# Delta-rule mixer of a three-block network on one core: chunks of 128 tokens in natural order instead of 64 folded ones

## The chip, the cores and the metric

The kernel runs on one core of one Trainium2 chip. The metric is the time of one execution of the whole program on the device, in microseconds (us); smaller is better. The program is written for the engines directly: every engine (TensorE = PE, VectorE = DVE, ScalarE = ACT, GpSimd = POOL, SyncE = SP) has its own list of instructions, carried out in that order, and semaphores join the lists. A wait in a list holds back all that stands behind it.

## The reference

The reference is a network of width 1024 on 256 tokens in float32: a block with a gated-delta-rule mixer and a mixture of 32 experts, then an "even" and an "odd" layer. The change touches only the first mixer. Its recurrence, run forward and, on reversed inputs, backward over the tokens, with 16 value heads of width 128 that share 8 query/key heads in pairs:

```python
def _gated_delta_rule(q, k, v, beta, g):
    """S_t = exp(g_t)(I - b_t k_t k_t^T) S_{t-1} + b_t k_t v_t^T ; o_t = S_t^T q_t.  Chunked WY form."""
    gc = jnp.cumsum(g, axis=-1)                       # within a chunk
    decay = jnp.exp(jnp.where(incl, gc[..., :, None] - gc[..., None, :], -jnp.inf))
    kb = k * beta[..., None]
    lhs = eye + jnp.einsum("nbhik,nbhjk->nbhij", kb, k) * decay * (1.0 - eye)
    u = solve(lhs, v * beta[..., None])               # unit lower triangular
    w = solve(lhs, kb * jnp.exp(gc)[..., None])
    attn = jnp.einsum("nbhik,nbhjk->nbhij", q, k) * decay
    def step(state, inp):                             # one chunk after the other
        v_new = u_c - w_c @ state
        o = q_c @ state + attn_c @ v_new
        state = state * gl[..., None, None] + k_c^T @ v_new
    ...
o = _gated_delta_rule(q, k, v, beta_f, g_f) + _rev(_gated_delta_rule(_rev(q), ..., _rev(g_b)))
```

q, k and v come from a projection of x, a convolution over 5 tokens and a silu; q and k are made unit vectors. The sum of both directions is normed, gated by silu(z) and projected by `w_out`. The reference cuts the sequence into chunks of 64; the result doesn't depend on the length of a chunk beyond rounding.

## The kernel before

The four stages `gdn`, `moe`, `even`, `odd` follow one another; the change is in `gdn`, the mixer. A head here is one of the 8 query/key heads with its two value heads. Every product is float32, and the profile counts each matmul as two instructions (a transpose as one).

**Tokens.** 256 tokens make 4 chunks of 64. Forward the order is 0, 1, 2, 3, backward 3, 2, 1, 0. Tokens are folded as 0, 3, 1, 2 (in the host's layout of xT and by `chunks` on ScalarE), so that a tile of 128 partitions holds two chunks, and one step of the recurrence takes the forward direction on one half of the partitions and the backward one on the other. A head has 4 such steps (`g.step`), the first with an empty state and the last without a new one.

**What one head costs on TensorE** (`gdn_tensor`, line 441): the projections, `project_half` (449), 12 parts of 4 matmuls, each 128x128 weights and 256 columns; the inverse of the unit triangular matrices by doubling: levels 1 to 4 join blocks of 1, 2, 4, 8 to 16 and 32 with products of 32x32 tiles, `level_y` (477) and `level_z` (500), 32 matmuls each; level 5 joins blocks of 32 to 64 with 16 each. Then the steps: `solve` (530) U = W^T R and `attend` (548), each 4 matmuls of 64x64 weights and 128 columns, 4 times; `add_state` (557), 4 of 64x128 weights and 128 columns, 3 times; `read_state` (520), 4 of 128x64 weights and 256 columns, 3 times. Also `keys` (591: k^T k, k^T q and the transposed keys), `unit_sums` (571), `turn_v` (583), and `turn_out` (605), which transposes the finished output of head h-2.

**Who serves it.** ScalarE (815): `keep_y` copies a level's y out of PSUM, `keep_u` U, `cross` writes level 5's block into W, `silu_v`, `keep_out`, `compact` (copies the diagonal 32x32 blocks of A = `g.at` next to each other), `decay` (the exponentials of the mask), `decay_state`. VectorE (1090): `update` X after each level (after level 4 it also turns X into W by 4 transposes, line 1178), `conv`, `bars` (log-decays less a mask), `triangles` (A = k^T k times decays), `attention`, `inverse_begin`, and in the steps `left`, `state`, `out`, `out_scale` (norm times gate, which `turn_out` waits for). GpSimd (1333) masks A for each level (line 1344).

**Order.** Written out by hand in each engine's loop over h. Iteration h carries the inverse of head h with the steps of head h-1 and `turn_out` of head h-2; the next head's q and k parts are projected two heads ahead. Between two products that depend on each other there stands mostly one projection part. At h = 6 there is no head h+2 left, so its last stretch has no projection. A ninth pass (h = 8) has the steps of head 7, with the first half of the output projection between them (`out_part`, line 787, 16 parts of 4 matmuls); `out_rest` follows (line 802). On VectorE `out_scale(h-2)` stands before `update(h, 4)` (lines 1311 to 1315).

**Queues.** All loads of weights are in SP's queue (`gdn_sync`, 373): units of 1 MB into a ring of 24 slots, each when its slot was used up (`fill`, 240); also the rows of cumulated log-decays, through DRAM (`rows_in`, 398). The experts' weights follow when a list of signals of the inverse is there (line 421).

Of the kernel before, what the change touches and what calls it, by code (L numbers as in the profile page):

```python
# [10 lines left out]
P = 128  # L11
# [94 lines left out]
def constants():  # L106
# [5 lines left out]
    half = P // 2  # L112
    same = i // half == j // half
    ci, cj = (r % half)[:, None], np.arange(half)[None, :]
    side = (r // half)[:, None]
    ordered = lambda before, w: np.where((side + w) % 2 == 0, before(ci, cj), before(cj, ci))

    def level(b):
        def before(u, v):
            return (u // (2 * b) == v // (2 * b)) & ((u // b) % 2 == 0) & ((v // b) % 2 == 1)  # L120
        return np.stack([ordered(before, w) for w in (0, 0, 1, 1)], 1)
# [4 lines left out]
    for w in POOL_WINDOWS:  # L126
# [18 lines left out]
        "eye2": ci == cj, "together": same,  # L145
        "upto": np.stack([ci <= cj, ci >= cj], 1), "behind": np.stack([ci > cj, ci < cj], 1),
        "bars": np.stack([~ordered(lambda u, v: u <= v, w) for w in (0, 0, 1, 1)], 1) * BIG,
        "eye32": (r % 32)[:, None] == np.arange(32)[None, :],
        "levels": np.stack([level(b) for b in LEVELS], 1).reshape(P, len(LEVELS), 4, 2, 32)[r, :, :, r // 32 % 2],
# [15 lines left out]
class Build:  # L165
    def __init__(self, nc, ins, out):
# [10 lines left out]
        self.delta_rows = nc.dram_tensor("delta_rows", (2, 4, QKH, P), F32, kind="Internal").ap()  # L177
# [115 lines left out]
    def gdn(self):  # L293
        al, g, new = self.alloc, Place(), self.signals.of
        H2, M8 = P // 2, [P, 2, 4, P // 2]
# [3 lines left out]
        g.eg, g.epsq = al("eg", [P, 2, 2, 2, VH]), al("epsq", [P, QKH, 2])  # L299
        late = QKH - 1  # L300
        g.cv, g.W, g.att, g.kk, g.vtm = [None] * 3, [None] * 3, [None] * 2, [None] * 2, [None] * 2
        shapes = (("cv", g.cv, [P, 2, T]), ("W", g.W, M8), ("att", g.att, M8), ("kk", g.kk, [P, 3, REP, P]),
# [5 lines left out]
        g.S, g.Sd = al("S", [P, 2, REP, P]), al("Sd", [P, 2, REP, P])  # L308
        g.R, g.U = al("R", [P, REP, P]), al("U", [P, REP, P])
        g.ost, g.junk = al("ost", [P, 4]), al("junk", [P, P])  # L310
        assert self.top <= ARENA - 9 * KT * UC
        for name, of, shape in shapes:
            for n in range(len(of)):
                if n != late % len(of):
                    of[n] = al(f"{name}{n}", shape)
# [9 lines left out]
        g.rowsb = pair("rows", [P, 512])  # L325
# [3 lines left out]
        g.dm, g.at = (al(n, M8) for n in ("dm", "at"))  # L329
        g.ac, g.mt, g.X, g.Y, g.Wc = (al(n, [P, 2, 4, 32]) for n in ("ac", "mt", "X", "Y", "Wc"))  # L330
        g.ktm = al("ktm", [P, 2, P])
# [4 lines left out]
        g.step = ((0, 0), (1, 0), (1, 1), (0, 1))  # L336
# [7 lines left out]
         g.ys, g.zx, g.zw, g.reads, g.us, g.avs, g.adds) = (  # L344
            new("PE", n) for n in ("gates", "gate_sums", "decays_turned", "q_projected", "v0_projected", "z0_projected",
                                   "unit_sums", "v_turned", "keys", "out_turned", "y_product",
                                   "zx_product", "zw_product", "state_read", "u_product", "attn_product",
                                   "state_added"))
        (g.gate_exps, g.gate_ln, g.gate_kept, g.cum_kept, g.qk_kept, g.vr_kept, g.qk_silu, g.v_silu, g.z_silu, g.squared, g.norm_ln, g.norms, g.rates_made, g.z_kept,
         g.v_kept, g.k_kept, g.decays, g.w_crossed, g.y_kept, g.u_kept, g.kk_made, g.s_decayed, g.out_squares, g.out_ln,  # L350
         g.out_norms, self.y_made) = (
            new("ACT", n) for n in ("gate_exps", "gate_ln", "gate_kept", "decays_kept", "qk_kept", "v_raw_kept", "qk_silu", "v_silu", "z_silu",
                                    "squared", "norm_ln", "norms", "rates_made", "z_kept", "v_kept", "k_kept", "decays", "w_crossed", "y_kept",
                                    "u_kept", "keys_scaled", "state_decayed", "out_squares", "out_ln", "out_norms", "y_made"))
# [10 lines left out]
        g.cleared2, g.masked, g.blank = (new("POOL", n) for n in ("w_cleared", "level_masked", "blank_made"))  # L365
# [7 lines left out]
    def gdn_sync(self, g):  # L373
# [19 lines left out]
        for x in range(2):  # L393
            SP.dma_start(self.delta_rows[x].rearrange("c h (v i) -> (c h v) i", v=REP),
                         g.crow[0:64, x * 64:(x + 1) * 64]).then_inc(*g.rows_out.up())
        SP.wait_ge(*g.rows_out(2))

        def rows_in(h):
            for x in range(2):
                SP.dma_start(g.rowsb[h % 2][g.halves[x]].rearrange("p (c n) -> p c n", c=4),  # L400
                             self.delta_rows[x:x + 1, :, h, :].to_broadcast([P // 2, 4, P])).then_inc(
                    *g.rows_in[h % 2].up())
# [18 lines left out]
        for done in (g.zw(QKH), g.w_crossed(QKH), g.v_turned(QKH), g.v_kept(QKH), g.kk_made(3 * QKH), g.x_made(9 * QKH),  # L421
                     g.masked(4 * QKH), g.attn_made(QKH)):
            SP.wait_ge(*done)
# [13 lines left out]
    def chunks(self, a, cc):  # L437

        return a.rearrange("p z (q i) -> p z q i", q=4)[:, :, cc:4 - cc:3 - 2 * cc, :]

    def gdn_tensor(self, g):
# [3 lines left out]
        chunk = lambda x, cc: slice(cc * P + x * 64, cc * P + x * 64 + 64)  # L445
# [31 lines left out]
        def level_y(h, l):  # L477


            if l == 1:  # L480
                M.wait_ge(*g.x_made(9 * h + 1))
                M.wait_ge(*g.k_kept(h + 1))
            else:
                M.wait_ge(*g.x_made(9 * h + 2 * l - 2))
            if l < 5:
                M.wait_ge(*g.masked(4 * h + l))
            for m in range(8):
                cc, w, n = m // 4, m % 4 // 2, slice(m * 32, m * 32 + 32)
# [4 lines left out]
                else:  # L493
                    for x in range(2):
                        a, b = w ^ x, 1 - (w ^ x)
                        q = M.matmul(ps[hq[2 * x + b], 3, n], g.at[hq[2 * x + a], cc, m % 4, 32 * b:32 * b + 32],
                                     g.X[hq[2 * x + a], cc, m % 4], start=True, stop=True, skip_group_check=True)
            q.then_inc(*g.ys.up())

        def level_z(h, l):  # L500
            M.wait_ge(*g.y_kept(5 * h + l))
            if l > 1:
                M.wait_ge(*g.x_made(9 * h + 2 * l - 1))
            elif h > 0:
                M.wait_ge(*g.w_crossed(h))
            for m in range(8):
                cc, w, n = m // 4, m % 4 // 2, slice(m * 32, m * 32 + 32)
# [4 lines left out]
                else:  # L512
                    for x in range(2):
                        a, b = w ^ x, 1 - (w ^ x)
                        q = M.matmul(ps[hq[2 * x + a], 4, n], g.Y[hq[2 * x + b], cc, m % 4],
                                     g.W[h % 3][hq[2 * x + b], cc, m % 4, 32 * b:32 * b + 32], start=True, stop=True,
                                     skip_group_check=True)
            q.then_inc(*(g.zx if l < 5 else g.zw).up())

        def read_state(h, n):  # L520
            cc, w = g.step[n]
            M.wait_ge(*g.s_kept(3 * h + n))
            for z in (1, 0):
                for x in range(2):
                    q = M.matmul(ps[hx[x], 6, (1 - z) * 256:(2 - z) * 256], g.cv[h % 3][:, z, chunk(x, cc)],  # L525
                                 g.S[:, w ^ x, :, :].rearrange("p v e -> p (v e)"), start=True, stop=True,
                                 skip_group_check=True)
            q.then_inc(*g.reads.up())

        def solve(h, n):  # L530
            cc, w = g.step[n]
            if n == 0:
                M.wait_ge(*g.x_made(9 * h + 9))
                M.wait_ge(*g.w_crossed(h + 1))
                M.wait_ge(*g.v_kept(h + 1))
                if h > 0:
                    M.wait_ge(*g.o_made(4 * h))
            else:
                M.wait_ge(*g.r_made(3 * h + n))
                M.wait_ge(*g.o_made(4 * h + n))  # L540
            for v in range(REP):
                for x in range(2):
                    rhs = g.vtm[h % 2][hx[x], cc, v, :] if n == 0 else g.R[hx[x], v, :]
                    q = M.matmul(ps[hx[x], 7, v * P:(v + 1) * P], g.W[h % 3][hx[x], cc, 2 * w + v], rhs, start=True,
                                 stop=True, skip_group_check=True)
            q.then_inc(*g.us.up())

        def attend(h, n):
            cc, w = g.step[n]
            M.wait_ge(*g.u_kept(4 * h + n + 1))  # L550
            for v in range(REP):
                for x in range(2):
                    q = M.matmul(ps[hx[x], 7, 256 + v * P:256 + (v + 1) * P], g.att[h % 2][hx[x], cc, 2 * w + v],
                                 g.U[hx[x], v, :], start=True, stop=True, skip_group_check=True)
            q.then_inc(*g.avs.up())

        def add_state(h, n):
            cc, w = g.step[n]
            if n > 0:
                M.wait_ge(*g.oq_made(3 * h + n))  # L560
            elif h > 0:
                M.wait_ge(*g.oq_made(3 * h))
            M.wait_ge(*g.kk_made(3 * h + n + 1))
            M.wait_ge(*g.u_kept(4 * h + n + 1))
            for v in range(REP):
                for x in range(2):
                    q = M.matmul(bank(5 + (w ^ x), P, v * P), g.kk[h % 2][hx[x], n, v, :], g.U[hx[x], v, :], start=True,
# [23 lines left out]
        def keys(h):  # L591
            cv = g.cv[h % 3]
            M.wait_ge(*g.qk_silu(h + 1))
            if h > 0:
                M.wait_ge(*g.y_kept(5 * h))
            for cc in range(2):
                M.transpose(bank(3, P, cc * P), cv[:, 1, tile(cc)], ident)
            for cc in range(2):
                for x in range(2):
# [2715 lines left out]
```

## Time and profile before

| | |
|---|---|
| median of 3 runs | 1098.59 us (1098.55 to 1101.07) |
| the profiled execution, its own time | 1099.91 us |
| its span, first to last instruction | 1098.6 us |
| TensorE busy | 1040.1 us, 95% of the span, 10605 matmul instructions |
| VectorE, ScalarE, GpSimd busy | 380.0, 353.3, 45.4 us |
| chain that ended last | PE 79%, SP's queue 12%, DVE 3%, ACT 3%, issue 2%, DMA 2% |
| mean granted clock of TensorE | 0.983 of full |

The chain is followed back from the last instruction. Busy time of matmuls is modelled at the ends, since they overlap; where a price is needed, the distance between the starts of two groups is the better measure. All rows below are of this one execution. The gdn stage is the first 403 us or so, the experts reach to about 670 us.

### The profile page before, as it was taken

How to read it: one execution, taken by the hardware profiler on the slowest of the kernel's cores; microseconds unless marked ns; L12 is line 12 of the kernel's file. 1: busy time of each engine (PE TensorE's matmuls, PEld its weight loads, DVE VectorE, ACT ScalarE, POOL GpSimd, SP SyncE). 2: the span in 40 equal slices, each digit the busy share in tenths (PEclk: the TensorE clock that was granted, in tenths of full speed). 3: DMA queues.
4: the chain of work that ended last, by engine and by line, in shares of the span. 5: the costliest groups of instructions: out<-in, count | busy, mean ns of one | idle time of the engine just before them, and what ended most of it. 6: DMA issues, size and time to landing. Idle time of an engine off the chain costs nothing.

```text
span 1098.6 us, 24280 instructions
## 1 busy us (share of the span) xinstructions
PE 1040.1 (95%) x10605; PEld 789.5 (72%) x10605; DVE 380.0 (35%) x942; ACT 353.3 (32%) x1006; POOL 45.4 (4%) x48
## 2 busy tenths in 40 slices
PE   9999999999989999889667899999999999999998
PEld 6777777777767787434333388888888888877787
DVE  2555556655644225101000234532000120065551
ACT  3555456555555232110000113022111331133550
POOL 0110010010000000000000000000000000024000
PEclk9999999999989999989888999999999999999999
DMA  7242232331323777999999953443444334472221
GB/s 282 57 162 83 92 131 80 120 131 75 118 81 121 299 306 281 398 421 420 423 422 423 406 230 137 155 154 115 153 153 153 135 121 149 136 249 77 78 77 39
DMA packets 41918, 209.84 MB, mean 191 GB/s; under 512 B 5184, under 2 KB 14272, under 8 KB 19024
## 3 DMA queue, kind: packets, MB, share of 16 engines
q1 hardware_dynamic: 41808, 208.25, 49.6%
q8 instruction: 85, 1.39, 0.5%
q14 instruction: 25, 0.20, 0.0%
HBM read 207.12 MB, written 1.11 MB: 190 GB/s over the span
## 4 chain that ended last, share of the span: by engine, by line
PE 79%; SPq 12%; DVE 3%; ACT 3%; issue 2%; DMA 2%; DVEq 0%; ACTq 0%
PE ps L2471 12%; PE ps L469 10%; SPq L245 9%; PE ps L2426 5%; PE ps L472 5%; PE ps L2310 4%; PE ps L2820 3%; PE ps L2885 3%; PE ps L797 3%; PE ps L2789 3%; PE ps L808 3%; PE ps L2135 3%; SPq L1494 2%; PE ps L525 2%; PE ps L491 2%; PE ps L510 2%
## 5 line engine op out<-in xcount | busy, mean ns | idle before, releaser
L2471 PE MATMUL ps<-slots,yt 128*128 128x256 f32 x608 | 131.8, 379 | 0.0
L469 PE MATMUL ps<-xt,slots 128*128 128x256 f32 x512 | 128.1, 396 | 0.9 <-issue 0.9
L2471 PEld LDWEIGHTS ps<-slots,yt 128*128 128x128 f32 x608 | 115.4, 190 | 15.6
L469 PEld LDWEIGHTS ps<-xt,slots 128*128 128x128 f32 x512 | 94.8, 194 | 21.3 <-issue 9.2
L472 PE MATMUL ps<-slots,xt 128*128 128x256 f32 x256 | 63.7, 392 | 0.5 <-issue 0.5
L2426 PE MATMUL ps<-slots,yt 128*128 128x256 f32 x256 | 56.6, 380 | 0.2
L1120 DVE SCALAR_TENSOR_TENSOR arena<-arena 128x256 f32<-128x256 f32 x128 | 56.2, 485 | 0.3
L472 PEld LDWEIGHTS ps<-slots,xt 128*128 128x128 f32 x256 | 46.1, 189 | 10.5 <-issue 4.3
L2426 PEld LDWEIGHTS ps<-slots,yt 128*128 128x128 f32 x256 | 48.1, 190 | 7.1 <-ACT yt L290 0.5
L1600 PE MATMUL ps<-arena 128*32 128x512 f32 x224 | 44.7, 620 | 7.9 <-DMA arena<-in_wu 6.3
L1600 PE MATMUL ps<-slots,arena 128*32 128x512 f32 x192 | 47.7, 643 | 1.9 <-DMA xt<-in_wu 1.9
L2310 PE MATMUL ps<-yt,slots 128*128 128x256 f32 x224 | 48.5, 379 | 0.0
L2310 PEld LDWEIGHTS ps<-yt,slots 128*128 128x128 f32 x224 | 42.5, 190 | 5.7
L3218 POOL TENSOR_TENSOR arena<-arena 128x512 f32<-128x512 f32 (+1 forms) x8 | 17.9, 2262 | 656.4 <-DVE arena L3101 656.4
L2525 ACT ACTIVATE arena<-ps,rms 128x256 f32<-128x256 f32 x32 | 13.4, 470 | 90.2 <-PE ps L2471 90.2
L2642 DVE SCALAR_TENSOR_TENSOR arena<-ps,arena 128x256 f32<-128x256 f32 x8 | 3.2, 478 | 108.5 <-ACT arena L2533 108.5
L1729 ACT ACTIVATE arena<-ps 128x256 f32<-128x256 f32 x8 | 3.1, 385 | 117.1 <-PE ps L1600 117.1
L1344 POOL TENSOR_TENSOR arena<-arena 128x256 f32<-128x256 f32 x32 | 25.4, 795 | 301.8 <-ACT arena L863 186.4
L1943 DVE TENSOR_TENSOR arena<-arena,ps 128x256 f32<-128x256 f32 x8 | 3.4, 422 | 95.0 <-ACT arena L1729 95.0
L1600 PEld LDWEIGHTS ps<-arena 128*32 128x32 f32 x224 | 11.6, 114 | 27.8 <-issue 27.8
L2820 PE MATMUL ps<-xt,slots 128*128 128x256 f32 x128 | 30.6, 385 | 0.6 <-ACT arena L3000 0.6
L797 PE MATMUL ps<-slots,yt 128*128 128x256 f32 x128 | 31.0, 389 | 0.0
(413 smaller groups left out, 1722.9 us busy)
## 6 DMA issues: line engine op xcount, KB each, us to landing
slots<-in_wu SPq DMA_DIRECT2D x107, 1024.0 KB, 4.9
arena<-in_wu SPq DMA_DIRECT2D x44, 1024.0 KB, 25.5
extra<-in_wu SPq DMA_DIRECT2D x12, 1024.0 KB, 21.0
yt<-in_wu SPq DMA_DIRECT2D x8, 1024.0 KB, 25.3
xt<-in_wu SPq DMA_DIRECT2D x4, 1024.0 KB, 27.6
arena<-in_wu SPq DMA_DIRECT2D x8, 512.0 KB, 8.2
extra<-in_wu SPq DMA_DIRECT2D x8, 512.0 KB, 17.0
arena<-bias_rows SPq DMA_DIRECT2D x1, 2048.0 KB, 14.0
```

Source lines behind the costliest of these rows:

```text
L245: SP.dma_start(self.slot(slot), self.ins["wu"][unit]).then_inc(*self.arrived[slot].up())
L469: q = M.matmul(bank(n, T), self.slots[:, s, k, n * P:(n + 1) * P], self.xt[:, k, :], start=(k == 0), stop=(k == KT - 1))
L472: q = M.matmul(bank(n, UC), folded(k, n), self.slots[:, s, k, :], start=(k == 0), stop=(k == KT - 1))
L797: q = M.matmul(self.out_bank(t, cg), self.yt[:, k, t * P:(t + 1) * P], self.slots[:, s, k, :], start=((cg % 2 == 0 or (t, cg) == (1, 3)) a ...
L808: q = M.matmul(self.out_bank(t, cg), self.yt[:, KT + k, t * P:(t + 1) * P], self.slots[:, s, k, :], start=False, stop=(k == KT - 1), skip_ ...
L1120: q = V.scalar_tensor_tensor(g.cn[:, s], src, w, g.cn[:, s], ALU.mult, ALU.add)
L1600: q = M.matmul(self.ps[r, 2, :], g.xg[:, half * (KT // 2) + k, r], self.flat(slots[e])[:, k * 512:(k + 1) * 512], start=(half == 0 and k = ...
L2135: q = M.matmul(self.bank(4 + cg, UC, t * UC), self.xt[:, k, t * P:(t + 1) * P], self.slot(s)[:, k, :], start=(t == 0 and k == 0), stop=(k ...
L2310: q = M.matmul(bank(s, T, T * n), self.slots[:, s, k, n * P:(n + 1) * P], self.xe[:, k, :], start=(k == 0), stop=(k == KT - 1), skip_group ...
L2426: q = M.matmul(bank(cg, UC, t * UC), self.yt[:, h * KT + k, t * P:(t + 1) * P], self.slots[:, s, k, :], start=(h == 1 and t == 0 and k == ...
L2471: q = M.matmul(self.bank(s, UC, t * UC), self.xe[:, k, t * P:(t + 1) * P], self.slots[:, s, k, :], start=(t == 0 and k == 0), stop=(k == K ...
L2820: q = M.matmul(bank(g.z_banks[u], T, n * T), self.slots[:, u, k, n * P:(n + 1) * P], self.xt[:, k, :], start=(n == 0 and k == 0), stop=(k ...
```

## The change

The chunk becomes 128 tokens in natural order: chunk 0 is tile 0, chunk 1 tile 1. Each direction has its own 128 partitions, so forward (d = 0) and backward (d = 1) are separate products of the whole array and a head has 2 steps (`place`) with one state in between, which starts from zero and so needs no decay. Triangular matrices are 128x128: `dm`, `at`, `att`, `W` and the decay rows double in width, and `dm`, `at`, two of the `W` and the rows move from the arena to the tiles `extra`. A sixth level, `join_y` and `join_z`, joins blocks of 64; `copy_x` on GpSimd (4 copies of 32 partitions) and two more pieces in `cross` assemble its operand `X64`, and `level_z` of level 5 has 8 more products of 32x32. The ninth pass is unrolled after the loop. The orders are written anew. The core of the diff (left out: constants, allocations, semaphore names, the copies that no longer fold):

```diff
         def level_z(h, l):
...
                 else:
+                    b = 1 + d
+                    M.matmul(ps[hq[b], 3, 256 + m * 32:288 + m * 32], g.W[h % 3][hq[b], cc, m % 4, 32 * b:32 * b + 32],
+                             g.Y[hq[b], cc, m % 4], start=True, stop=True, skip_group_check=True)
...
+        def join_y(h):
+            M.wait_ge(*g.x_crossed(h + 1))
+            M.wait_ge(*g.w_crossed(h + 1))
+            M.wait_ge(*g.x_copied(h + 1))
+            for m in range(4):
+                for d in range(2):
+                    q = M.matmul(ps[hx[1 - d], 4, 256 + m * 64:320 + m * 64],
+                                 g.at[hx[d], cc, 2 * d + v, 64 * (1 - d):64 * (2 - d)], g.X64[hx[d], cc, v], start=True,
+                                 stop=True, skip_group_check=True)
+        def join_z(h):
+            M.wait_ge(*g.y_kept(6 * h + 6))
+            for m in range(4):
+                for d in range(2):
+                    q = M.matmul(ps[hx[d], 4, m * 64:m * 64 + 64], g.Y64[hx[1 - d], cc, v],
+                                 g.W[h % 3][hx[1 - d], cc, 2 * d + v, 64 * (1 - d):64 * (2 - d)], start=True, stop=True,
+                                 skip_group_check=True)
+        def read_state(h):
             for z in (1, 0):
+                for d in range(2):
+                    q = M.matmul(bank(5 + d, 256, (1 - z) * 256), g.cv[h % 3][:, z, tile(1 - d)],
+                                 g.S[:, d].rearrange("p v e -> p (v e)"), start=True, stop=True, skip_group_check=True)
         def solve(h, n):
...
+            for d in range(2):
+                for v in range(REP):
+                    cc = g.place(d, n)
+                    rhs = g.vtm[h % 2][:, cc, v, :] if n == 0 else g.R[:, d, v, :]
+                    q = M.matmul(bank(7, P, (2 * d + v) * P), g.W[h % 3][:, cc, 2 * d + v], rhs, start=True, stop=True,
+                                 skip_group_check=True)
...
         def keys(h):
...
             for cc in range(2):
+                M.matmul(bank(3, 256, cc * 256), cv[:, 1, tile(cc)], cv[:, :, tile(cc)][:, ::-1], start=True, stop=True,
+                         skip_group_check=True)
             for cc in range(2):
+                q = M.transpose(bank(7, P, cc * P), cv[:, 1, tile(cc)], ident)
```

`attend` (2 per head) and `add_state` (1) are 4 matmuls of 128x128 weights and 128 columns too. TensorE's loop, new (conditions left out; `part(i)` is a half of a projection):

```text
level_y 1, solve(h-1,0), part, level_z 1, attend(h-1,0), add_state(h-1), part, level_y 2, part, level_z 2,
read_state(h-1), part, level_y 3, part, level_z 3, solve(h-1,1), part, level_y 4, unit_sums(h+1), attend(h-1,1),
part, level_z 4, part, level_y 5, turn_out(h-2), part of h+2, level_z 5, part of h+2, join_y, keys(h+1),
part of h+2, join_z, turn_v, part of h+2
```

The end of the other engines' loops:

```diff
 VectorE
             conv(h, 1, 1)
             update(h, 4)
+            if h > 1:
+                out_scale(h - 2)
+            conv(h, 1, 2)
+            conv(h, 1, 3)
+            conv(h, 1, 4)
             if ahead:
                 triangles(h + 1)
                 attention(h + 1)
                 inverse_begin(h + 1)
 ScalarE
             cross(h)
             silu_v(h)
             if h > 1:
                 keep_out(h - 2)
+            if next_half:
                 keep_qk(h + 2, 0)
+            keep_join(h)
             if ahead:
+                keep_k(h + 1)
                 compact(h + 1)
+            join(h)
             keep_v(h)
 GpSimd
             for l in range(1, 5):
                 mask(h, l)
+            copy_x(h)
 SP (rows_in: one transfer of 128 partitions x 4 KB in place of two of 64 x 2 KB)
```

`copy_x` waits for the fourth transpose of `update(h, 4)`. At the start `keys(0)` is followed by 8 products (64x128 weights, 128 columns) that spread head 0's decay rows, in place of 16 of 64x64 weights and 64 columns.

## Rows read from the trace of the kernel before

**Rows 1.** Busy by stretch: span, PE, PEld, DVE, ACT, POOL busy, clock, DMA share, GB/s.

```profile
181.60:223.00 41.40, 41.10 (x837) 31.32 (x836) 24.26 (x63) 23.58 (x76) 3.15 (x4) 1.00 0.31 111
486.00:610.00 124.00, 96.58 (x668) 44.07 (x666) 12.39 (x24) 11.22 (x25) 0.00 (x0) 0.92 1.01 421
```

**Rows 2.** TensorE's timeline, steady iterations: start, duration, line, shape, idle before.

```profile
194.04 0.66 PE L553 MATMUL ps<-arena 64*64 64x128 f32 x8
194.63 0.71 PE L567 MATMUL ps<-arena 64*128 64x128 f32 x8
195.27 1.99 PE L469 MATMUL ps<-xt,slots 128*128 128x256 f32 x8
197.20 0.75 PE L491 MATMUL ps<-arena 32*32 32x32 f32 x64
197.88 1.08 PE L525 MATMUL ps<-arena 128*64 128x256 f32 x8
198.90 1.99 PE L469 MATMUL ps<-xt,slots 128*128 128x256 f32 x8
...
219.65 1.08 PE L525 MATMUL ps<-arena 128*64 128x256 f32 x8 [0.30 <-DVE arena L1212]
```

**Rows 3.** TensorE's timeline elsewhere: small products, two parts in a row, full products of 128 columns.

```profile
25.64 1.15 PE L661 MATMUL ps<-arena,cst 64*64 64x64 f32 x32
...
364.86 3.72 PE L797 MATMUL ps<-slots,yt 128*128 128x256 f32 x16
368.51 1.08 PE L525 MATMUL ps<-arena 128*64 128x256 f32 x8
...
429.43 3.84 PE L1576 MATMUL ps<-arena,x 128*128 128x128 f32 x32 [0.78 <-DVE arena L1925]
```

**Rows 4.** Timelines: VectorE's triangles and out_scale; level_z 4 on TensorE and what follows on VectorE.

```profile
183.06 0.69 DVE L1147 TENSOR_TENSOR arena<-ps,arena 128x512 f32<-128x512 f32 x1 [2.55 <-PE ps L601]
...
211.55 1.13 DVE L1233 SCALAR_TENSOR_TENSOR arena<-arena 128x128 f32<-128x128 f32 x4
...
215.03 0.75 PE L510 MATMUL ps<-arena 32*32 32x32 f32 x64
...
215.83 0.42 DVE L1169 TENSOR_TENSOR arena<-arena,ps 128x256 f32<-128x256 f32 x1 [2.36 <-PE ps L510]
216.29 1.79 DVE L1178 STREAM_TRANSPOSE arena<-arena 32x256 f32<-32x256 f32 x4
```

**Rows 5.** A VectorE line's durations (min/median/max ns), and GpSimd's mask beside one of them.

```profile
L1156 DVE TENSOR_TENSOR arena<-arena x8: 427/832/839, 32.6 to 311.1; 128x256 f32<-128x256 f32 x8
...
187.68 0.97 POOL L1344 TENSOR_TENSOR arena<-arena 128x256 f32<-128x256 f32 x1 [23.50 <-ACT arena L863]
```

**Rows 6.** ScalarE's timeline in the stretch from level 5 to the next head.

```profile
182.14 1.12 ACT L876 ACTIVATE arena<-ps 32x128 f32<-32x128 f32 x4 [1.28 <-PE ps L515]
183.29 0.84 ACT L999 ACTIVATE yt<-ps,arena 128x256 f32<-128x256 f32 x2
...
185.89 1.71 ACT L863 ACTIVATE arena<-arena 32x256 f32<-32x256 f32 x4
```

**Rows 7.** TensorE's timeline: head 6 begins, hands over to head 7, its level 4, the end of the ninth pass.

```profile
274.04 0.75 PE L491 MATMUL ps<-arena 32*32 32x32 f32 x64
...
312.09 1.08 PE L491 MATMUL ps<-arena 32*32 32x32 f32 x64 [2.37 <-DVE arena L1159]
...
314.15 3.53 PE L469 MATMUL ps<-xt,slots 128*128 128x256 f32 x8
...
338.93 0.75 PE L510 MATMUL ps<-arena 32*32 32x32 f32 x64
...
388.83 7.93 PE L808 MATMUL ps<-slots,yt 128*128 128x256 f32 x36
```

**Rows 8.** TensorE's timeline in the experts: idles of 2 us and what follows.

```profile
560.56 3.64 PE L1640 MATMUL ps<-extra,arena 128*32 128x512 f32 x32 [2.20 <-DMA extra<-in_wu]
...
590.37 5.30 PE L1640 MATMUL ps<-arena 128*32 128x512 f32 x32 [2.01 <-DMA arena<-in_wu]
```

More of the change, by code:

```diff
@@ L110, in constants @@
     eye = (i == j).astype(np.float32)
[L112 to L116, printed above, removed]
+    ordered = lambda before, d, u, v: before(u, v) if d == 0 else before(v, u)
+    ri, rj = (r % 32)[:, None], np.arange(32)[None, :]
     def level(b):
@@ L546, in solve @@
             q.then_inc(*g.us.up())
         def attend(h, n):
[L549 to L554, printed above, removed]
-            q.then_inc(*g.avs.up())
[L557 to L567, printed above, removed]
+            M.wait_ge(*g.u_kept(2 * h + n + 1))
@@ L677, in gdn_tensor @@
+        for h in range(QKH):
+            step, ahead, next_half = h > 0, h + 1 < QKH, h + 2 < QKH
+            level_y(h, 1)
             if step:
                 solve(h - 1, 0)
-            if step and level:
                 project_half(h, 2, 0)
-            if level:
-                level_z(h, 1)
-            if last:
-                self.out_part(0, 2)
+            level_z(h, 1)
             if step:
                 attend(h - 1, 0)
-                add_state(h - 1, 0)
-            if step and level:
+                add_state(h - 1)
@@ L728, in gdn_tensor @@
[L728 to L743 removed]
+            project_half(h, 5, 0)
@@ L767, in gdn_tensor @@
                 self.out_part(0, 1)
-            if level:
-                turn_v(h)
-            if h + 2 < QKH:
+            join_z(h)
+            turn_v(h)
+            if next_half:
                 project_half(h + 2, 1, 1)
-            if last:
-                self.out_part(3, 2)
-                self.out_part(3, 3)
+            elif not ahead:
+                self.out_part(0, 2)
+        h = QKH - 1
+        solve(h, 0)
+        self.out_part(0, 3)
+        attend(h, 0)
+        add_state(h)
@@ L775, in gdn_tensor @@
+        self.out_part(1, 0)
+        self.out_part(1, 1)
+        read_state(h)
+        self.out_part(1, 2)
+        turn_out(h - 1)
+        self.out_part(1, 3)
+        solve(h, 1)
+        self.out_part(2, 0)
+        attend(h, 1)
+        for part in range(1, 4):
+            self.out_part(2, part)
+        for part in range(4):
+            self.out_part(3, part)
         M.wait_ge(*self.y_made(2 * QKH - 2))
@@ L1276, in gdn_vector @@
         inverse_begin(0)
-        for h in range(QKH + 1):
-            level, step, ahead = h < QKH, h > 0, h + 1 < QKH
+        for h in range(QKH):
+            step, ahead = h > 0, h + 1 < QKH
             if ahead:
@@ L1281, in gdn_vector @@
                 conv(h + 1, 0, 1)
[L1282 to L1284 removed]
+            update(h, 1)
             if ahead:
```

586 lines of the change are left out of this document (257 added, 329 removed).

## The prediction, made before the changed kernel was run

> **What bounds the kernel now.** I read first the busy time by stretch. In a steady iteration of the mixer's loop TensorE is busy 41.10 of 41.40 us, VectorE 24 and ScalarE 24 [rows 1]. So an iteration is as long as TensorE's list, and it shortens only by what leaves that list, as long as each wait in it stays covered. Next TensorE's timeline: the reader sees products of head h between projection parts, start to start 0.59 us for a solve or attend (194.04 to 194.63), 0.64 for an add_state, 1.02 for a read_state, 1.92 for a part, 0.68 for a level product, and one idle of 0.30 a head, before the third read_state [rows 2]. Last the stretches behind: the experts' middle moves 421 GB/s at a DMA share of 1.01 [rows 1], so there TensorE waits for weights. The stream is fed as slots come free behind the mixer's end; I take a shift of that end to pass on whole, since the queue is filled by TensorE's progress until then. The other bound is that a little of a gain is lost there.
>
> Everything below is a difference in us against the profiled execution, whose own time is 1099.9 (span 1098.6); the median of the runs is 1.3 lower.
>
> **1. Products of one steady head.** Removed: 4 solves and 4 attends at 0.59, 3 add_states at 0.64, 3 read_states at 1.02 [rows 2]: 4.72 + 1.92 + 3.06 = 9.70. Added: 2 solves, 2 attends, 1 add_state, each 8 instructions of 128x128 weights and 128 columns. That very shape ran 32 in 3.84 us, 0.11 each without the last one's tail and 0.12 with it [rows 3]; 8 make 0.92, five groups 4.6. The read_state is a part's shape: 1.73 (two parts in a row took 3.65, the first 1.92, so the second 1.73 [rows 3]). The 0.19 is what a full product pays behind small tiles. Five parts that stood behind small tiles now stand behind full products, and five of the new groups stand behind small tiles, so it cancels in the loop. Joins: 16 instructions of 64x64 weights and 64 columns each, by 32 in 1.15 [rows 3] 0.54 each with the tail off, 1.08; by the 128-column solve [rows 2] it would be 2.4 at most. Level 5 has 8 more small products, 8/32 of 0.68: 0.17. Keys: two full products of 256 columns (0.86) for four half ones (taken as a solve's 0.59): +0.3. Sum: -9.70 + 4.6 + 1.73 + 1.08 + 0.17 + 0.3 = **-1.8**, and -0.3 for the idle before the third read_state, which no longer exists: **-2.1 a head** where the steps run (h = 1 to 6). At h = 0 there are only the additions, +1.55.
>
> **2. turn_out waits for out_scale (stall A).** TensorE calls turn_out(h-2) straight behind level_y 5. It waits for out_scale(h-2), which VectorE now has behind all of update(h, 4), where it used to stand before it. From the start of level_z 4 at 215.03: the subtraction starts 0.80 later, the four transposes end at 218.08, that is +3.05, and out_scale takes 1.13 [rows 4]: +4.2. TensorE is there after 0.68 for level_z 4, 1.92 for a part and 0.4 for level_y 5: +3.0. Stall 1.2. Nothing can cover it: what follows on TensorE stands behind the wait. Beside out_scale runs the new copy_x, released by the same fourth transpose. When GpSimd's mask runs beside VectorE, a VectorE instruction of two SBUF operands takes 0.83 where it takes 0.43 alone (median and minimum), and the mask 0.97 [rows 5]. out_scale has two such operands, four times; copy_x has four copies. No row shows a copy of 32 partitions x 128 elements; between nothing and a whole mask of 0.97 each I take 0.25, since a copy has an eighth of a mask's elements: +0.9 if each copy blocks one step. **A = 2.1**, at h = 2 to 7; bounds 1.2 and 4.
>
> The Trainium skill, page "SBUF — State Buffer", section "SBUF: two separate sides", says that VectorE with two SBUF inputs and GpSimd take one pair of ports in turn, each for its whole instruction. By it A is the 2.1; with no such rule it would be the 1.2. The pair 0.43 and 0.83 agrees with it.
>
> **3. From keys to the next level_y 1 (stall B).** Count from the start of join_y. TensorE: 0.54, keys 1.1 + 0.19, a part 1.77, join_z 0.54, turn_v 0.63, a part 1.77: at +6.55 it wants level_y(h+1, 1). VectorE's triangles doubles: 0.42 for 256 and 0.69 for 512 elements [rows 4] give 1.23 for 1024. So A is made at 0.54 + 1.1 + 0.3 + 1.23 = +3.15. compact stands on ScalarE behind cross (now 6 pieces at 0.28, 0.57 + 0.2 after level_z 5 starts), silu_v with its table load (about 1.9), keep_out (0.75), keep_qk, keep_join and keep_k (0.28 each) [rows 6]: +3.45. compact takes 1.71 [rows 6], and inverse_begin about 1.85 more: +7.0. **B = 0.5** at h = 2 to 5, about 0.2 at h = 0 and 1, where keep_out is missing. join_y waits for all of cross: 0.78 + 1.7 = 2.5 after level_z 5 starts, while level_z 5 and one part take 2.5: no stall while a part stands there. join_z's copy is ready at +3.2, TensorE comes at +3.6. The mask for level 1 (0.97) fits under inverse_begin.
>
> **4. The start.** Before head 0's inverse nothing covers the chain: the spread of the decay rows has full-width outputs (16 instructions at 0.11, 1.75, for 1.07), keys +0.25, bars and triangles +0.53 each, eight exponentials of 128 columns +0.4: **+2.4**.
>
> **5. Head 6 to 7.** No parts of a head h+2 are left. Before: 312.09 - 274.04 = 38.05 [rows 7]. After: 24.9 to level_z 4 (as before within 0.2), +5.1 to turn_out, +0.5 to level_z 5, then cross bare (2.55), A at +3.15 after that, compact, inverse: 9.3 in all: 39.8, **+1.75**. The clock had fallen here before: the part at 314.15 took 3.53 for 1.92 [rows 7]. With more idle I add **+1.0**.
>
> **6. Head 7 and the last steps.** From level_z 4 of head 7 to the first out_rest it was 388.83 - 338.93 = 49.9 [rows 7], with three quarters of the 9.70 plus the last head's 9.70. After: A and turn_out 5.6, to join_y 2.55, from there to turn_v and a part 6.1 (join_z waits 0.7 for its copy), five groups of 0.9, a read_state, thirteen more output parts at 1.73 (all now stand behind full products) and a turn_out: 43.6. **-6.3**.
>
> **7. Waits moved, taken as nothing.** bars(h+1) now stands behind left(h-1), some 13 us later. SP waits for it before rows_in(h+2) and fill(1), so the v weights of the next head start some 2 us later than their slot is free; they have 20 us. The rows are twice the bytes, one transfer; DMA is at 0.31 of its engines [rows 1]. Bounds of both: nothing. scale_keys and squares on ScalarE keep their place. If the cover were gone, a late weight would cost its lateness once a head.
>
> **Sum without the clock:** start +2.4; h = 0 +1.75; h = 1 -1.9; h = 2 to 5 (-2.1 + 2.1 + 0.5) x 4 = +2.0; h = 6 +2.75; h = 7 and the rest -6.3: **+0.7**. Products alone would give about -12: the stalls eat it.
>
> **8. The clock.** An idle of 2 us was followed once by full speed (3.64) and once by a cold stretch (5.30 for the same 32 instructions) [rows 8], so a fall costs 1.6 and comes in some of such idles. Stall A is such an idle, and small products stand before it. I take two falls in the five iterations not yet counted: **+3.3**. Together +4.0: 1103.9 by the profiled execution, **1102.6** as a median.
>
> **Rivals.**
> - *Stall A is only the order (1.2) and the clock holds.* GpSimd's copies are short and don't block. Then -0.9 x 6 and no clock term: 0.7 - 5.4 = -4.7: 1093.9, faster. For it: 560.56, where 2.20 idle cost nothing [rows 8]. Against: [rows 5]. 0.27.
> - *The clock falls in each iteration behind stall A.* 5 x 1.65 = +8.2 on +0.7: +8.9, 1107.5; with the copies nearer to a mask's length some 5 more, 1112. For it: 312.09 and 590.37 [rows 7, 8]. The point from which it decides: when A passes 2 us. 0.15.
> - *Full products of 128 columns are bound by their weights' load and cost as much as a part's instructions* (0.22 for 0.11 [rows 2, 3]): 40 groups x 0.9 = +34, 1136. Against it is the shape's own row [rows 3]. 0.05.
>
> **How the numbers follow.** About 0.3%, 3.3 us, is what a measurement of this kernel can tell from no change. The forecast has 0.53, its own range -2 to +9 (copies 0 to 0.5 each, no to five falls): of it 0.24 is slower, 0.25 same, 0.04 faster, since +4.0 lies close to the bound. The first rival gives 0.24 faster and 0.03 same, the other two 0.20 slower. Faster 0.28, same 0.28, slower 0.44. Range: the first rival's time less 2 to the second's upper end: 1092 to 1112; outside it are the third rival and a tail below.
>
> **What would show it.** In the changed profile: solve and attend groups at 0.9, read_state 1.7 to 1.9 each once a head; turn_out's transposes with an idle of 2 us before them, released by out_scale, at h = 2 to 7; level_y 1 with 0.5 idle released by inverse_begin's transpose; level_y 1 of head 0 starting 2.4 later than before; part groups of 3.5 us where the clock fell; out_rest's start 1 to 5 us later than 388.8. It is wrong if turn_out has no idle (then 1088 or less), or if the loop's iterations come out near 39.

## The result and the profile of the changed kernel

The changed kernel took 1108.01 us in the median of four runs (1103.91 to 1108.88), the kernel before 1099.83 beside it (1098.55 to 1101.63): ratio 1.0066, 95% interval 1.0035 to 1.0097. It is slower, by some 8 us, where the prediction had 4. The profiled execution is the fastest of its four, 1103.91 with a span of 1102.6, against 1098.6 before: +4.0. The two traces are compared on that; what it leaves out of the 8 comes up at the third experiment.

First TensorE's timeline of the changed kernel in head 4, an attend and an add_state behind each other, and then the middle of the head (start, duration, line; the idle before it in brackets):

```profile
200.05 1.16 PE L577 MATMUL ps<-arena 128*128 128x128 f32 x8
201.05 1.06 PE L588 MATMUL ps<-arena 128*128 128x128 f32 x8
201.94 1.89 PE L465 MATMUL ps<-xt,slots 128*128 128x256 f32 x8
...
215.72 1.16 PE L565 MATMUL ps<-arena,extra 128*128 128x128 f32 x8
216.72 1.89 PE L468 MATMUL ps<-slots,xt 128*128 128x256 f32 x8
218.54 1.08 PE L486 MATMUL ps<-arena 32*32 32x32 f32 x64
...
222.73 0.75 PE L505 MATMUL ps<-arena 32*32 32x32 f32 x64
223.42 1.99 PE L468 MATMUL ps<-slots,xt 128*128 128x256 f32 x8
225.34 0.47 PE L491 MATMUL ps<-arena,extra 32*32 32x32 f32 x32
227.32 0.66 PE L636 MATMUL ps<-cst,arena 128*128 128x128 f32 x4 [1.50 <-DVE arena L1204]
...
232.14 0.68 PE L526 MATMUL ps<-arena,extra 64*64 64x64 f32 x16
232.75 1.13 PE L622 MATMUL ps<-arena 128*128 128x256 f32 x4
```

A solve (line 565) takes 1.00 from start to start behind small tiles, a part behind it 1.82, a join (line 526) 0.61. An add_state (588) behind another full product takes 0.89. turn_out (636) stands 1.50 behind level_y 5 (491) and is released by out_scale (1204). This is stall A. The same idle stands there at all six heads that have a turn_out in the loop. VectorE and GpSimd around it:

```profile
223.53 0.42 DVE L1152 TENSOR_TENSOR arena<-arena,ps 128x256 f32<-128x256 f32 x1 [0.62 <-PE ps L505]
223.99 1.79 DVE L1160 STREAM_TRANSPOSE arena<-arena 32x256 f32<-32x256 f32 x4
225.81 1.45 DVE L1204 SCALAR_TENSOR_TENSOR arena<-arena 128x128 f32<-128x128 f32 x4
...
225.84 1.28 POOL L1304 COPY arena<-arena 32x128 f32<-32x128 f32 x4 [11.15 <-DVE arena L1160]
```

The order is as read: subtraction, four transposes, out_scale, with the copies beside it. out_scale takes 1.45 where it took 1.13 [rows 4]. Now the waits of TensorE, summed over the mixer's stage, first before, then changed (line, who it waited for: us in total, times, longest):

```profile
PE ps L491 <- DVE arena L1159: 2.4, 1, 2.4
PE ps L525 <- DVE arena L1212: 2.1, 7, 0.3
...
PE ps L510 <- issue: 1.3, 2, 0.9
...
PE ps L469 <- issue: 0.9, 1, 0.9
...
PE ps L472 <- issue: 0.5, 1, 0.5
```

```profile
PE ps L636 <- DVE arena L1204: 9.0, 6, 1.5
PE ps L486 <- DVE arena L1142: 5.4, 8, 2.2
PE ps L505 <- issue: 3.4, 2, 1.8
PE ps L546 <- issue: 2.1, 1, 2.1
PE ps L526 <- issue: 1.8, 1, 1.8
...
PE ps L577 <- issue: 1.5, 1, 1.5
...
PE ps L486 <- issue: 0.4, 1, 0.4
```

Two things were forecast: 9.0 us before turn_out, and 5.4 before level_y 1 (line 486; the start, small ones, and 2.2 where head 6 hands over). "issue" is an idle in which TensorE waited for nothing the profile shows: 2.7 us before, 9.2 now. Of the six idles five stand in the middle of a group of equal instructions. The sixth, 1.8 us, stands before a whole group, join_y of head 6, and is no idle of this kind. join_y waits for ScalarE's `cross` (line 871), and cross ends just there:

```profile
315.26 1.11 ACT L871 ACTIVATE extra<-ps 32x128 f32<-32x128 f32 x4
...
316.47 0.68 PE L526 MATMUL ps<-arena,extra 64*64 64x64 f32 x16 [1.83 <-issue]
```

In experiments 1, 2, 5 and 6 the profile names cross as the releaser at the same place. Head 6 has no part there, so this is the bare cross that the prediction counted with. What is left for "issue" is 7.4 us, 4.7 more than before.

What TensorE waits for in the other five can be seen. The trace also holds every DMA packet with its queue, size, start and duration; no view above prints them. Its queue 8 (kind "instruction" on the page) carries 85 packets of 16 KB. The five idles end at 84.19, 132.80, 199.87, 208.29 and 286.69, and each time such a packet started 2.2 to 2.5 us earlier and took 0.9. It is so in the mixer's stage of all ten traces: at every idle of TensorE over 0.25 us put down to issue, but those before join_y, the last instruction packet started 2.2 to 2.7 us earlier (once 3.1). Before join_y it was 6.1. So in these idles TensorE waits for instructions. The packets were not slow, they started late.

Where the four us lie is read from the starts of level_y 1 of the heads. Before, 34.00, 64.52, 105.53, 148.72, 190.13, 231.53, 274.04, 312.09; now 36.46, 69.53, 110.92, 152.66, 193.81, 239.07, 280.41, 323.90. So the start costs +2.46; the iterations of heads 0 to 6 +2.55, +0.38, -1.45, -0.26, +3.86, -1.17, +5.44. From there to level_z 4 of head 7 it is -0.59, and from there to the first out_rest, which now starts at 392.78 for 388.83 [rows 7], -7.27. Together +3.95. The expensive iterations hold the idles put down to issue: head 4 has 1.85 and 1.53, head 6 has 1.49, head 1 has 2.12. Without them and those of before, the iterations of heads 1, 2, 3 and 5 are 0.3 to 1.7 us shorter than before, that of head 4 is 0.5 longer.

Behind the mixer nothing changed: the first products of the experts' last step start at 630.53 instead of 626.38, and the end is 4.0 later. The shift passes on whole, as taken.

### The profile page after: what moved, and what is told of

It is laid out like the page before. It is cut to its first block, busy times and chain, and to the rows that moved or that the text cites. A ratio compares the mean times of both kernels' runs of the same rounds, so it can differ in the third digit from the quotient of the medians.

```text
span 1102.6 us, 23717 instructions
## 1 busy us (share of the span) xinstructions
PE 1031.3 (94%) x10409; PEld 804.2 (73%) x10409; DVE 374.3 (34%) x877; ACT 341.9 (31%) x900; POOL 62.8 (6%) x81
## 4 chain that ended last, share of the span: by engine, by line
PE 76%; SPq 12%; ACT 4%; DVE 4%; issue 3%; DMA 1%; POOL 0%; ACTq 0%; DVEq 0%; POOLq 0%
PE ps L2443 12%; SPq L241 10%; PE ps L465 7%; PE ps L2398 5%; PE ps L2282 4%; PE ps L468 4%; PE ps L2792 3%; PE ps L2857 3%; PE ps L2761 3%; PE ps L794 3%; PE ps L2107 3%; PE ps L783 2%; PE ps L486 2%; SPq L1466 2%; PE ps L505 2%
## 5 line engine op out<-in xcount | busy, mean ns | idle before, releaser
L2443 PE MATMUL ps<-slots,yt 128*128 128x256 f32 x608 | 131.8, 379 | 0.0
L465 PE MATMUL ps<-xt,slots 128*128 128x256 f32 x512 | 125.0, 390 | 0.0
L2398 PE MATMUL ps<-slots,yt 128*128 128x256 f32 x256 | 56.6, 380 | 0.2
L1314 POOL TENSOR_TENSOR arena<-arena 128x256 f32<-128x256 f32 x32 | 31.0, 970 | 220.8 <-PE ps L486 125.7
L1152 DVE TENSOR_TENSOR arena<-arena,ps 128x256 f32<-128x256 f32 x32 | 13.5, 423 | 70.7 <-PE ps L505 70.7
L1915 DVE TENSOR_TENSOR arena<-arena,ps 128x256 f32<-128x256 f32 x8 | 3.4, 422 | 92.9 <-ACT arena L1701 92.9
L486 PEld LDWEIGHTS ps<-arena 32*32 32x32 f32 x2048 | 21.6, 108 | 18.0 <-DVE arena L1142 8.6
L505 PEld LDWEIGHTS ps<-arena 32*32 32x32 f32 x2048 | 21.1, 106 | 14.8 <-issue 14.2
## 6 DMA issues: line engine op xcount, KB each, us to landing
extra<-delta_rows SPq DMA_DIRECT2D x7, 512.0 KB, 11.4
```

Source lines behind the costliest of these rows:

```text
L465: q = M.matmul(bank(n, T), self.slots[:, s, k, n * P:(n + 1) * P], self.xt[:, k, :], start=(k == 0), stop=(k == KT - 1))
L486: q = M.matmul(ps[p, 3, n], g.mt[p, cc, m % 4], g.X[p, cc, m % 4], start=True, stop=True, skip_group_check=True)
L505: q = M.matmul(ps[p, 4, n], g.Wc[p, cc, m % 4], g.Y[p, cc, m % 4], start=True, stop=True, skip_group_check=True)
L2398: q = M.matmul(bank(cg, UC, t * UC), self.yt[:, h * KT + k, t * P:(t + 1) * P], self.slots[:, s, k, :], start=(h == 1 and t == 0 and k == ...
L2443: q = M.matmul(self.bank(s, UC, t * UC), self.xe[:, k, t * P:(t + 1) * P], self.slots[:, s, k, :], start=(t == 0 and k == 0), stop=(k == K ...
```

## The experiments

**The theory after the profile:** three separate costs, stall A, late instructions behind the transfers of the decay rows (the page has 512 KB a head in pieces of 1 KB, where 256 KB in pieces of 512 bytes were), and the uncovered stretches at the start and at head 6. **The rival:** one cost that is seen in several places (the phase of the loop, or the clock), so that taking away one stall moves it elsewhere.

Each experiment ran beside the kernel before. The changed kernel has only its own four runs, taken beside the kernel before at another time. So a distance to its 1108.0 is best read as a difference of two ratios to the kernel before, and then has a 95% interval of some 3.5 to 4 us either way: experiment 1 is 10 us below it, experiment 2 is 4, experiment 3 is 8.

### 1. out_scale before level 4's update

```diff
+            if h > 1:
+                out_scale(h - 2)
             update(h, 4)
-            if h > 1:
-                out_scale(h - 2)
```

> The changed kernel with out_scale(h-2) moved before update(h, 4) on VectorE, nothing else. Theory (turn_out's wait is made by the order of VectorE's list): the six idles of 1.5 us before turn_out go, level_y 1's small idles stay, time about 8 to 9 us below the changed kernel's. Rival (PE is held by something else there, and the stall moves to the next product): the idle turns up before level_z 5 or join_y and the time moves by less than 3 us.

1096.61 us, ratio to the kernel before 0.9974 (0.9958 to 0.9989), so 11.4 below the changed kernel and, alone, already faster than the kernel before. TensorE's timeline of this run:

```profile
220.45 0.75 PE L505 MATMUL ps<-arena 32*32 32x32 f32 x64
221.13 1.99 PE L468 MATMUL ps<-slots,xt 128*128 128x256 f32 x8
223.06 0.47 PE L491 MATMUL ps<-arena,extra 32*32 32x32 f32 x32
223.46 0.66 PE L636 MATMUL ps<-cst,arena 128*128 128x128 f32 x4
```

turn_out follows level_y 5 with no idle. The order made the stall, and where parts follow it doesn't move on. At the two last heads a little of it does: 0.8 us before level_z 5 of head 7, and join_y of head 6 now waits 2.5 for cross instead of 1.8:

```profile
PE ps L526 <- ACT extra L871: 2.5, 1, 2.5
```

The spans of the two profiled executions differ by 8.9 us, and the six stalls were 9.0. The rest of the 11.4 is within the interval of the difference.

### 2. copy_x behind out_scale

```diff
             G.wait_ge(*g.x_made(9 * h + 9))
+            if h > 1:
+                G.wait_ge(*g.o_scaled(h - 1))
```

> The changed kernel with GpSimd's copy_x held back until out_scale(h-2) is done. Theory (1.2 of the 1.5 us are VectorE's order, 0.3 is GpSimd beside it): idle before turn_out 1.2 instead of 1.5, time 1 to 2 us lower, within what can be measured. Rival (GpSimd has no part): idle stays 1.5.

```profile
L1204 DVE SCALAR_TENSOR_TENSOR arena<-arena x32: 347/349/355, 139.0 to 387.3; 128x128 f32<-128x128 f32 x32
...
PE ps L636 <- DVE arena L1204: 7.1, 6, 1.2
```

In the changed kernel the first row reads:

```profile
L1204 DVE SCALAR_TENSOR_TENSOR arena<-arena x32: 347/406/465, 139.4 to 387.5; 128x128 f32<-128x128 f32 x32
```

The median of an out_scale instruction falls from 406 to 349 ns, and the idle from 1.50 to 1.19. GpSimd's part is 0.3 us a head, as expected from the difference of the rows. The time, 1103.3 (ratio 1.0029, 1.0013 to 1.0046), fell by more than the 1 to 2 us expected, but with that interval the two can't be told apart; the 1.9 us that the idles give are what is shown.

### 3. The decay rows in pieces of 4 KB

```diff
-  (1, 4, QKH, REP * P)
+  (1, QKH, 4, REP * P)
...
-            SP.dma_start(g.rowsb[h % 2].rearrange("p (c n) -> p c n", c=4),
-                         self.delta_rows[0:1, :, h, :].to_broadcast([P, 4, REP * P]))
+            SP.dma_start(g.rowsb[h % 2],
+                         self.delta_rows[0, h:h + 1].rearrange("a c n -> a (c n)").to_broadcast([P, 4 * REP * P]))
```

> The changed kernel with the decay rows laid out in DRAM so that a partition's 4 KB are one piece instead of four of 1 KB. Theory (TensorE's idles put down to issue, 9.2 us in the loop, come from instructions that arrive late behind the rows' small packets): these idles fall to some 3 us, as in the kernel before, time about 5 us lower. Rival (they are the weights' transfers or chance): they stay at 6 to 10 us and the time does not move.

1099.35 us, ratio 0.9991 (0.9979 to 1.0003): 8.7 below the changed kernel. (The edit also writes the rows out in four transfers in place of one.) Time and idles agree with the theory: without the 1.82 before join_y, which is cross again, 3.6 of the 7.4 us are left (0.29, 1.86, 1.49), where 3 were expected. What changed is seen in stretches of 2 us of the changed kernel and of this one (the last three columns are the granted clock, the DMA engines' busy share and GB/s):

```profile
198.00:200.00 2.00, 0.15 (x7) 0.13 (x5) 0.00 (x0) 0.00 (x0) 0.00 (x0) 1.00 1.04 434
200.00:202.00 2.00, 2.00 (x23) 1.96 (x20) 1.63 (x4) 0.00 (x0) 0.00 (x0) 1.00 0.86 164
202.00:204.00 2.00, 2.00 (x37) 1.51 (x40) 1.86 (x4) 0.13 (x1) 0.00 (x0) 1.00 0.90 69
204.00:206.00 2.00, 2.00 (x67) 1.80 (x54) 0.22 (x1) 0.64 (x2) 0.73 (x1) 1.00 0.94 57
206.00:208.00 2.00, 0.76 (x27) 0.32 (x25) 0.00 (x0) 0.00 (x0) 0.00 (x0) 1.00 0.12 21
```

```profile
196.00:198.00 2.00, 1.00 (x12) 0.96 (x12) 0.67 (x2) 0.00 (x0) 0.00 (x0) 0.94 0.97 403
198.00:200.00 2.00, 2.00 (x11) 2.00 (x11) 0.97 (x3) 0.00 (x0) 0.00 (x0) 0.50 0.33 129
200.00:202.00 2.00, 2.00 (x9) 1.73 (x8) 1.50 (x3) 0.00 (x0) 0.00 (x0) 0.70 0.00 0
```

In the changed kernel the rows keep the DMA engines 0.9 busy for some 5 us while they move 57 to 69 GB/s. That is after the weights, which fill them at 430. Of TensorE's two idles at head 4 the first stands beside the weights, the second at the rows' end. The rows' 1 KB packets start from 200.17 to 206.46, and the instruction packet that ends the second idle starts at 206.10; at head 1 the rows start from 75.92 to 81.86, and the packet at 81.72. With long pieces this tail is gone, and so is the second idle; the first stays, and a cold stretch follows it here (clock 0.50). The two idles that disappear (2.1 at head 1, 1.5 at head 4) are 3.6 us of the 4.4 by which the profiled executions differ. The changed kernel's profiled execution is 4.1 below its own median, so its trace may show less of this than its other runs had; that is not shown.

### 4. The rows sent twice

```diff
+            spare = self.extra[:, 3]...[:, h % 2 * 1024:h % 2 * 1024 + 1024]
+            SP.dma_start(spare.rearrange("p (c n) -> p c n", c=4),
+                         self.delta_rows[0:1, :, h, :].to_broadcast([P, 4, REP * P])).then_inc(*g.rows_in[h % 2].up())
```

> The changed kernel with each transfer of decay rows made twice, the second into tiles that nobody reads. Theory (rows' packets delay TensorE's instructions): idles put down to issue grow from 9 to some 15 us, time 5 us or more above the changed kernel's. Rival (weights' transfers or chance): within 2 us of it.

1158.5 us, ratio 1.053 (1.0512 to 1.0548): 50 above the changed kernel for seven transfers of 512 KB more. (VectorE waits for both transfers of a head here.) TensorE's waits:

```profile
PE ps L489 <- issue: 33.3, 5, 12.9
PE ps L639 <- DVE arena L1207: 9.0, 6, 1.5
PE ps L549 <- issue: 8.2, 1, 8.2
PE ps L508 <- issue: 7.5, 2, 5.4
```

With 1.7 more, and without the 1.8 before join_y, some 51 us are put down to issue where the changed kernel has 7.4, and stall A is the same 9.0. That is 43 of the 56 us between the two profiled executions. The mean granted clock is also lower, 0.956 for 0.975, which may be the rest. Some idles stand where they did, before the same products: 8.2 us in read_state of head 1, where it was 2.1. Others are new, the longest, 12.9 us, in a level_y of head 0. This is the strongest evidence that the rows' small pieces hold back TensorE's instructions. The packets show it too. At the six longest idles the last of the rows' 1 KB packets starts at 52.48, 102.48, 154.15, 202.42, 251.38 and 306.45, and the instruction packet starts at 51.45, 102.28, 153.26, 202.17, 251.29 and 305.98, each time 0.1 to 1.0 us before the last of the rows. So it comes when the rows are through. When it was asked for, and where it waited, the trace does not show.

### 5. Both edits

out_scale first, as in 1, and rows of 4 KB, as in 3.

> The changed kernel with both edits, out_scale before update(h, 4) and the rows as one piece of 4 KB a partition. Theory (two separate costs, turn_out's wait and late instructions behind the rows' packets, that add up): 11.4 and 8.7 us below the changed kernel's 1108.0 give together some 1088 us, 1% faster than the kernel before. Rival (they are the same cost seen twice, the clock or the phase of the loop): no better than 1096.

1091.91 us, ratio 0.9913 (0.9893 to 0.9932), some 8 to 9 us faster than the kernel before and 16 below the changed one. The costs are separate. They don't add up to the full 20.1 (1088), but that sum leans twice on the changed kernel's four runs: by the ratios the two edits give 0.92% and 0.75%, and both together 1.53%, which is their sum within the noise. This version beats both kernels.

### 6. Both, and the rows in mid-iteration

```diff
+            if h + 2 < QKH:
+                SP.wait_ge(*g.barred(h + 1))
+                rows_in(h + 2)
             if h + 3 < QKH + 1:
                 self.fill(0, ...)
```

> As e5, and SP sends the rows after the z weights in the middle of an iteration, not in one go with three units of weights. Theory (what delays the instructions is a full queue, rows and weights together): idles put down to issue fall from some 5 us to 3 or less, 1 to 3 us below e5. Rival (place in the queue does not matter, weights alone do it): same as e5 within 1 us.

1091.19 us, ratio 0.9914 (0.9895 to 0.9934), the same as experiment 5. The rows land in 6.2 us instead of 8.9, but the idles put down to issue stay: 0.56 at head 0, 1.85 at head 4, 1.49 at head 6. The rival held here. What is left of these idles stands beside the weights' transfers, and the place of the rows doesn't matter once their pieces are long.

### 7 and 8. The kernel before, with long rows, and with its rows twice

In 7 the four pieces of 512 bytes a partition become one of 2 KB, as in 3. In 8 each of the two transfers a head is made twice, the second into tiles that nobody reads, as in 4.

> The kernel before with its decay rows laid out as one piece of 2 KB a partition in place of four of 512 bytes. Theory (the rows' packets delay TensorE's instructions there too, 2.7 us of idles put down to issue in its loop): these fall, time 1 to 3 us lower. Rival (the kernel before is not touched by it): no difference.

> The kernel before with each transfer of decay rows made twice, the second into tiles that nobody reads; so it moves as many packets as the changed kernel moves bytes in. Theory (the number of small packets counts; twice the rows of before are 1024 pieces of 512 bytes a head): issue idles grow from 2.7 to 10 us or more, time 7 us or more above the kernel before. Rival (it is something of the new TensorE order): less than 3 us.

Long rows leave the kernel before where it was: 1100.67 us, ratio 1.0003 (0.999 to 1.0016). Its few idles of this kind (0.39, 0.40, 0.66 and 1.85 in this run) are not the rows'. Twice the rows cost it 17 us: 1117.32, ratio 1.0161 (1.0133 to 1.0189). Its idles put down to issue are 13.3 us, and its waits show where the longest stand:

```profile
PE ps L496 <- issue: 5.2, 2, 4.4
PE ps L515 <- issue: 3.9, 2, 3.0
PE ps L549 <- issue: 2.8, 1, 2.8
```

So it is no property of the new order on TensorE. The rows cost the kernel before nothing as they were and 17 us when made twice; how much it takes in between, no run shows.

## Why the prediction was right, and where it was not

The direction and the main mechanism were right: the products save time, stall A and the uncovered stretches eat it. That the profiled execution came out at +3.95 for a forecast of +4.0 is luck, as the steps show; the medians are 8 apart.

1. **Products.** -2.1 a head was forecast. The iteration of head 5, with no idle put down to issue, is TensorE busy 39.53 us where it was 41.10 [rows 1]: -1.6, and -0.3 for the idle that is gone, as forecast. A solve between small tiles and a part is 1.00, in a run of full products 0.89; the forecast's 0.92 lies between.
2. **Stall A**, forecast 2.1, measured 1.50, and 1.19 with GpSimd out of the way. The part from the order was exact (1.2). GpSimd's was mis-sized: its copies take 0.29 us each, but out_scale lost only 0.3 in all, not one copy's length at each step. The rule of the shared ports in the Trainium skill (page "SBUF — State Buffer", section "SBUF: two separate sides") agrees in kind, since the loss goes when the copies wait. It does not agree in size: out_scale (1.45) and the copies (1.28) ran side by side from 225.8, while one at a time they would need 1.13 and four times 0.29, some 2.3 in all. The measurement decides, with the reserve that durations on GpSimd are rough.
3. **Stall B**, forecast 0.5, measured 0.2 to 0.3.
4. **The start**, forecast +2.4, measured +2.46. Head 0 behind it was forecast at +1.75 and came to +2.55; the clock stayed low there for 6.7 us (see 8), before for 3.2.
5. **Head 6 to 7**, forecast +1.75 and +1.0 for the clock; measured +5.44, of which 1.49 is an idle put down to issue. The 1.83 before join_y is the bare cross, which was in the forecast: join_y starts 2.5 after level_z 5, as forecast (2.55). What is left is 3.95, in place of 2.75, though stall A is 0.6 shorter. The clock term was too small: a fall behind the late instructions and a longer one at the end stand in 8. (The forecast's "sum without the clock" has this 1.0 of clock in it.)
6. **The last steps**, forecast -6.3, measured -7.3: TensorE's part, as stall A is shorter by 0.6 there.
7. **Waits moved, taken as nothing: this step failed.** "The rows are twice the bytes, one transfer; DMA is at 0.31 of its engines [rows 1]. Bounds of both: nothing." The share was a mean over the iteration. In the few us in which rows and weights are in flight it is 0.9 to 1.0 at head 4, and then TensorE's instructions come late: 7.4 us of such idles for 2.7, +4.7 in the profiled execution, and more in the median if experiments 3 and 4 are a measure. Of the 7.4, 3.6 stand behind rows and go with long pieces; the rest stands beside weights or x. This was the missing term.
8. **The clock.** Falls behind stall A were forecast, +3.3. There were none. In the changed kernel, a stretch of head 0, one behind an idle put down to issue at head 4, one behind stall A of the same head, one behind an idle put down to issue at head 6, and the handover to head 7 (columns: span, PE, PEld, DVE, ACT, POOL busy, clock, DMA share, GB/s):

```profile
37.60:44.30 6.70, 5.98 (x136) 4.56 (x136) 2.52 (x7) 1.99 (x4) 1.67 (x2) 0.51 0.02 5
208.29:212.00 3.71, 3.71 (x55) 3.29 (x56) 2.82 (x9) 1.37 (x3) 0.00 (x0) 1.00 0.02 4
227.30:231.30 4.00, 3.98 (x65) 3.36 (x66) 2.34 (x6) 1.35 (x6) 0.00 (x0) 1.00 0.55 229
...
286.70:290.70 4.00, 4.00 (x17) 3.79 (x18) 1.04 (x2) 0.00 (x0) 0.00 (x0) 0.57 0.06 22
317.50:327.60 10.10, 7.40 (x100) 5.95 (x99) 4.06 (x5) 6.42 (x17) 1.69 (x2) 0.51 0.07 29
```

The clock stayed at its full level (2.4 GHz) in the 4 us behind each of the six stalls A; at head 6 it fell after them, behind the bare cross. It also stayed there behind the late instructions of 2.12, 1.85 and 1.53 us. It was at the lower level (1.2 GHz) for most of the stretch behind the 1.49 us at head 6, where an add_state took 1.71 for 0.89:

```profile
287.71 1.91 PE L588 MATMUL ps<-arena 128*128 128x128 f32 x8
289.42 2.36 PE L465 MATMUL ps<-xt,slots 128*128 128x256 f32 x8
```

So the length of an idle alone does not say here whether the clock falls. At head 0 and at the handover the clock was low in the kernel before too, but for 3.2 and 6.7 us, where it is now 6.7 and 10.1. In all it was low for some 10 us more of the mixer's stage, at places where the forecast had only 1.0.

So the forecast's total was near for a partly wrong reason: two terms were too high (A by 3.6, the falls behind it by 3.3), one was missing (the late instructions, 4.7), and the clock at head 0 and head 6, less a gain in the last steps, holds the 2 that are left.

Of the rivals, the first (the order's 1.2 alone, the clock holds) described stall A and the clock better than the forecast did, and still the kernel is slower, since what it left out is what the forecast left out too. The second and the third fell: no fall behind stall A, and full products of 128 columns cost 0.11 an instruction. (The third's 40 groups at 0.9 are 36, where it has 34.)

## What to carry to other kernels

When a product is made larger and fewer, look in the other engines' lists for what its consumer waits for: a step that used to stand before a long block and now stands behind it (here out_scale behind level 4's update) can cost all that the products save, and moving it back costs nothing. A transfer is to be judged by its pieces and by the busy share in the microseconds in which it is in flight, not by bytes and the mean. After a layout change, idles that the profile puts down to issue, in the middle of equal instructions, are worth comparing with those of before. One that stands before a whole group is first to be held against what that group waits for in the code, as join_y against cross here.

## What the runs showed of the hardware

I had not expected that a transfer of 512 KB, read from one place of DRAM into 128 partitions in pieces of 1 KB, keeps the DMA engines 0.9 busy at 57 to 69 GB/s for some 5 us, as at head 4. The weights' transfers run at 430 GB/s at about the same share. The rate is much the same at the other heads looked at, 61 to 75 GB/s at head 1, but the share isn't: 0.28 to 0.59 there. Nor had I expected that a second transfer of this kind a head costs a TensorE-bound kernel 50 us, most of it in idles for which the profile names no releaser, up to 12.9 us in one place, while twice the rows in pieces of 512 bytes cost the kernel before 17. In all traces TensorE goes on 2.2 to 2.7 us after an instruction packet of 16 KB started, with one exception (3.1), and behind the rows this packet starts only with the last of the rows. What the weights do to it stays open: an idle of 1.5 to 2.2 us stands beside them at head 4 in every version of the new order, and no kernel took the weights away.
